# Hybrid SSD / gated-DeltaNet encoder block on one core: SBUF buffers moved to offsets that are multiples of 256 bytes

## What is computed

```python
h = rms_norm(x, g_mix_pre)
proj = h @ w_in                        # 1024 -> 8224 columns: z, xbc, dt, qkv, gate, b, a, m_gate
y_ssm = mamba2_branch(z, xbc, dt, ...)          # causal conv, silu, chunked scan
y_gdn = gdn_branch(qkv, gate, b, a, ...)        # causal conv, silu, l2 norm, chunked delta rule
mixed = sig(mg0) * (y_ssm @ w_br_ssm) + sig(mg1) * (y_gdn @ w_br_gdn)
x = x + rms_norm(mixed @ w_out, g_mix_post)
h = rms_norm(x, g_ffn_pre)
act = gelu(causal_dwconv(h @ w_ffn_gate, conv_ffn_w) + conv_ffn_b)
x = x + rms_norm((act * (h @ w_ffn_up)) @ w_ffn_down, g_ffn_post)
e = sigmoid(x @ w_ple_gate) * (p @ w_ple_proj)
out = x + rms_norm(e, g_ple_post)
```

## Time and profile before

| | |
|---|---|
| median of 3 runs | 2702.46 us (2697.34 to 2707.08) |
| the profiled execution | 2704.22 us, of which the span from first to last instruction 2702.4 us |
| PE busy | 2580.7 us, 95% of the span, 12044 matmuls |
| weight loads (PEld) | 2115.2 us, 78% |
| DVE / ACT / POOL busy | 1468.1 / 531.8 / 1069.9 us |
| DMA | 304.58 MB, 113 GB/s over the span |
| mean granted TensorE clock | 0.98 |

### The profile page before, as it was taken

The page is one execution under the profiler, slowest core; times in us unless marked ns, Lnnn a source line. Parts: engine busy times, 40 slices in busy tenths (PEclk is TensorE's granted clock), DMA queues, the critical chain, the costliest instruction groups (busy, mean ns, idle before and its releaser), DMA issues. The chain is left out here.

```text
span 2702.4 us, 29575 instructions
## 1 busy us (share of the span) xinstructions
PE 2580.7 (95%) x12044; PEld 2115.2 (78%) x12044; DVE 1468.1 (54%) x1172; ACT 531.8 (20%) x550; POOL 1069.9 (40%) x549
## 2 busy tenths in 40 slices
PE   6999999799989999979998799999999999999998
PEld 5888888577778888768876588888888888888776
DVE  4779776234665567731426744444444444444675
ACT  4100101455412323230014200000000000000332
POOL 2334332365435555523365433333333333333353
PEclk8999999899999999999998899999999999999999
DMA  5222222699856575553243211111111111111132
GB/s 200 101 100 87 101 94 78 178 266 289 255 163 204 159 211 163 169 163 133 98 143 101 94 47 47 47 47 47 47 47 47 47 47 49 54 53 62 63 109 101
DMA packets 277598, 304.58 MB, mean 113 GB/s; under 512 B 43837, under 2 KB 241802, under 8 KB 273418
## 3 DMA queue, kind: packets, MB, share of 16 engines
q1 hardware_dynamic: 246778, 249.40, 30.1%
q10 hardware_dynamic: 30736, 54.01, 5.5%
HBM read 216.87 MB, written 86.51 MB: 112 GB/s over the span
## 5 line engine op out<-in xcount | busy, mean ns | idle before, releaser
L440 PE MATMUL ps<-act_hi,w_hi 128*128 128x512 f32 x2288 | 912.9, 399 | 22.6 <-ACT ring_b L920 12.4
L443 PE MATMUL ps<-act_lo,w_hi 128*128 128x512 f32 x2288 | 898.4, 393 | 0.0
L444 PE MATMUL ps<-act_hi,w_lo 128*128 128x512 f32 x2288 | 896.8, 392 | 0.0
L425 POOL TENSOR_SCALAR w_hi<-w_raw 128x1024 fp32r<-128x1024 f32 x219 | 251.7, 1149 | 1429.6 <-PE ps L440 605.4
L427 POOL TENSOR_TENSOR w_lo<-w_raw,w_hi 128x1024 fp32r<-128x1024 f32 x219 | 582.8, 2661 | 18.3
L440 PEld LDWEIGHTS ps<-act_hi,w_hi 128*128 128x128 f32 x2288 | 431.5, 189 | 123.8 <-ACT ring_b L920 15.5
L444 PEld LDWEIGHTS ps<-act_hi,w_lo 128*128 128x128 f32 x2288 | 430.8, 188 | 95.9
L443 PEld LDWEIGHTS ps<-act_lo,w_hi 128*128 128x128 f32 x2288 | 431.6, 189 | 92.6 <-issue 3.4
L2097 DVE TENSOR_TENSOR tile<-ps,tile 128x1024 f32<-128x1024 f32 x112 | 135.7, 1221 | 107.8 <-PE ps L1626 106.5
L2527 DVE SCALAR_TENSOR_TENSOR ring_a<-xin,par,ring_a 128x1024 f32<-128x1024 f32 x108 | 185.1, 1714 | 11.8 <-DVE ring_a L2521 0.3
L1625 PE MATMUL ps<-f_lo,w_hi 128*128 128x512 f32 x480 | 189.1, 394 | 0.0
(11 more groups left out here) (303 smaller groups left out, 2912.6 us busy)
## 6 DMA issues: line engine op xcount, KB each, us to landing
w_raw<-in_w_in_dram SPq DMA_DIRECT2D x34, 1024.0 KB, 5.4
spill<-ring_b ACTq DMA_DIRECT2D x67, 512.0 KB, 2.7
w_raw<-in_w_ffn_gate_dram SPq DMA_DIRECT2D x17, 1024.0 KB, 5.4
w_raw<-in_w_ffn_up_dram SPq DMA_DIRECT2D x17, 1024.0 KB, 5.4
w_raw<-in_w_ffn_down_dram SPq DMA_DIRECT2D x16, 1024.0 KB, 4.9
qkv_a<-spill SPq DMA_DIRECT2D x8, 1536.0 KB, 12.5
dec_a<-cum_rows SPq DMA_DIRECT2D x16, 512.0 KB, 13.9
gdn_in<-hrow SPq DMA_DIRECT2D x8, 1024.0 KB, 11.9
```

Source lines behind the costliest of these rows:

```text
L425: nc.gpsimd.tensor_scalar(hi, raw, 1.0, 0.0, ALU.mult, ALU.add).then_inc(split_done, 1)
L440: first = nc.tensor.matmul(o, wh, mov[0][:, k, c], start=(k == 0), stop=False)
L443: nc.tensor.matmul(o, wh, mov[1][:, k, c], start=False, stop=False)
L444: last = nc.tensor.matmul(o, wl, mov[0][:, k, c], start=False, stop=(k == KD - 1))
```

## The change

Only the order and number of SBUF allocations change; no instruction is added, removed or moved on any engine, apart from the addresses.

1. `w_raw`, `w_hi`, `w_lo` are allocated after the small constants instead of before them; `hv` moves from the head of the mixer's stack to the constants; an unused tensor `fill` of 32 bytes follows.
2. An unused tensor `fill_x` of 224 bytes follows `xin`.
3. `orst` moves from the middle of the chunk loop's buffers to their end.

```diff
@@ -64,14 +64,16 @@
-    w_raw = sb("w_raw", [P, 2, 2048])
-    w_hi = sb("w_hi", [P, 2, 1024], f32r)
-    w_lo = sb("w_lo", [P, 2, 1024], f32r)
     ident = sb("ident", [P, P])
     ones = sb("ones", [P, P])
     eps_t = sb("eps_t", [P, 1])
     par = sb("par", [P, 4, P])
     d_ch = sb("d_ch", [P, KD])
+    hv = sb("hv", [P, 4])
+    fill = sb("fill", [P, 8])
+    w_raw = sb("w_raw", [P, 2, 2048])
+    w_hi = sb("w_hi", [P, 2, 1024], f32r)
+    w_lo = sb("w_lo", [P, 2, 1024], f32r)
@@ -122,7 +124,6 @@
     ph12 = ExitStack()
-    hv = sb("hv", [P, 4], f32, ph12)
     m_incl = sb("m_incl", [P, P], f32, ph12)
@@ -144,6 +145,7 @@
     xin = sb("xin", [P, 2, SEQ + 4], f32, sub)
+    fill_x = sb("fill_x", [P, 56], f32, sub)
     hrow = sb("hrow", [P, 4, SEQ], f32, sub)
@@ -176,12 +178,12 @@
     yssm = sb("yssm", [P, KD, P], f32, ph2)
-    orst = sb("orst", [P, GDN_HEADS], f32, ph2)
     xbc = sb("xbc", [P, XBC_T, P], f32, ph2)
     nt = sb("nt", [P, GDN_HEADS, P], f32, ph2)
     dd = sb("dd", [P, 2 * GDN_HEADS, P], f32, ph2)
     rinv = sb("rinv", [P, GDN_HEADS, P], f32, ph2)
     xinv = sb("xinv", [P, GDN_HEADS, P], f32, ph2)
+    orst = sb("orst", [P, GDN_HEADS], f32, ph2)
```

## The result

The changed kernel takes 2684.34 us (median of 5 runs, 2676.67 to 2688.19) against 2702.70 us of the kernel before in the same session (5 runs, 2697.34 to 2707.08). A later session gave 2679.98 against 2701.77 us.

What follows compares the result with a forecast made beforehand. PE was taken as the bound, busy 2580.7 of 2702.4 us. No instruction is added or moved and every address term was taken as 0, so 2702.5 + 0 = 2702.5 us, range 2692 to 2710.

Steps and rivals of the forecast that it cites:

- PE's reads: Matmul operand reads: new start addresses change nothing, 0 us, with bounds of -176 us and its mirror.
- B: All float32r matmuls: reads run faster at 0 because PE's two reads meet less often, -176 us, 2526; chance 0.03.
- Rival D: Float32r matmuls: slower at 0, with weights and moving operand at one remainder, up to 2879 us; chance 0.02.
- DVE: Convolution taps reading `xin`: offset does nothing, 0 us, all staying at 1283 to 1285 ns.
- ACT and POOL: Operations of these engines: 0 us, lower end -1 us; durations stay with their lines, not with the offset.
- DMA, stores: 512 KB stores out of `ring_b` and `hrow`: 0 us, both landing after 2.6 us whatever the offset.
- DMA, loads: Loads into `xbc`, `gt`, `dec`: taken as 0; a misaligned target costs at most 0.4 of 4.3 us, 9%.
- Rival A: Chunk loop: transfers at remainder 224 pay for it and the change removes that, -9 us, 2693; chance 0.09.
- The seam: Between Z stretch and chunk loop: PE's 7.54 us wait unchanged, 0 us, ends -7.5 and +5.9 us.
- rival C: Seam gets longer: `sub_n` lands 5.9 us later and the clock stays down longer, +9.5 us, 2712; chance 0.06.
- faster: Whole kernel: time measurably below no change, by about 0.3%, 8 us; chance 0.11.

Runs made afterwards that it cites:

- loop_at_0: Kernel before with only the buffers of the epilogue (`ring_a`, `ring_b`, `xin`) and of the chunk loop moved to 0: 2700.46 us, ratio 0.9986.
- the direct comparison above: Changed kernel beside the changed kernel without its 32-byte filler (all buffers at 224), on one chip: 2679.98 against 2687.85 us.

## Why the prediction was wrong, step by step

**The step that failed** is the first term, *PE's reads*: "I take 0: the float32 rows are nearest, being the same engine, the same two reads and the same change of remainder." In its place the runs show 2.22 ns less per float32r matmul, 228.89 to 226.67, set by the difference of the two starts. The nearest rival was B, given 0.03: it had the sign, and a start address as the cause. But its condition, an operand at 0, isn't the one that counts (both at 128 or 224 do as well), its size was off (19 ns per matmul), and that PE's two reads meet, as it said, fits all runs but was not isolated. The row that the prediction named for B showed it: 4148 starts in the 940 us, where "right" was 4108, give or take 3. Three things were wrong in that step.

*The wrong variable.* The step compared remainders (`dd`, `nt` at 0 with `rhs`, `mq` at 224), but each of these pairs has equal remainders, so the difference was 0 in both rows that it compared. They could not show what 64 bytes between the operands cost. Rival D even named the fact ("now at one remainder instead of 64 bytes apart") and gave it the wrong sign. By the runs, in cycles at 2.4 GHz per matmul of 512 columns:

| moving operand minus weights, mod 256 | 0 | 32 | 64 | 96 | 128 | 160 | 192 | 224 |
|---|---|---|---|---|---|---|---|---|
| cycles | 544 | 560 | 549.3 (at times 560) | 560 | 558 or 560, by stretch | 562.3 | 560 | 560 |

So the kernel before was already in the second-best place, and the change brought it to the best.

*The wrong neighbour.* Float32 matmuls are not like float32r ones here. In the trace after, sixteen of either pair still take 1.95 us, and four of 512 columns 1.88, as in the earlier trace rows. One of these rows says more than the prediction took from it: `s_ssm` lay at 224 and `xbc` at 0 and both are at 0 now, so this float32 pair did change its difference, and its time stayed. Other float32 pairs of 512 columns (`hrow`, `ones` and `fa`, `ones`) cover the remaining differences in the traces, 0 to 224 in steps of 32, and take 428.7 to 429.9 ns in the mean at each.

```profile
852.86 1.88 PE L831 MATMUL ps<-s_ssm,xbc 128*128 128x512 f32 x4
...
868.85 1.95 PE L778 MATMUL ps<-rhs,mq 128*128 128x128 f32 x16
...
875.09 1.95 PE L778 MATMUL ps<-dd,nt 128*128 128x128 f32 x16
```

The float32 one spends about 0.43 us on 512 columns, 1.9 times the time of the float32r one, so it takes in its columns at about half the rate.

*A row that was at hand and not read.* The trace of before holds float32r matmuls at both levels of the clock, right behind the seam's wait; start us, us, instruction:

```profile
790.51 0.63 PE L443 MATMUL ps<-act_lo,w_hi 128*128 128x512 f32 x1
790.94 0.63 PE L444 MATMUL ps<-act_hi,w_lo 128*128 128x512 f32 x1
791.37 0.63 PE L440 MATMUL ps<-act_hi,w_hi 128*128 128x512 f32 x1
791.79 0.63 PE L443 MATMUL ps<-act_lo,w_hi 128*128 128x512 f32 x1
792.22 0.63 PE L444 MATMUL ps<-act_hi,w_lo 128*128 128x512 f32 x1
...
792.99 0.39 PE L443 MATMUL ps<-act_lo,w_hi 128*128 128x512 f32 x1
793.22 0.39 PE L444 MATMUL ps<-act_hi,w_lo 128*128 128x512 f32 x1
```

At the lower level, 1.2 GHz (granted clock 0.50 from 790.5 to 792.3 us), four spacings take 792.22 - 790.51 = 1.71 us, 0.427 us each: 512 cycles for 512 columns, nothing on top. At 2.4 GHz it is 549.3 cycles. A clock twice as fast makes the matmul only 1.86 times as fast, so 37 cycles, 15.5 ns, of every matmul were not column work at its rate at the lower level. That is a sign that something other than the array sets the pace, and by it the most that a layout can give is, as an estimate, 9552 * 15.5 ns = 148 us, from a measurement instead of the guessed "half the cost per column". After the change 32 of the 37 cycles are still there. In the kernel with weights at 0 alone, 560 cycles at the upper level, the lower one shows the same 0.427 us (803.91 - 799.64 = 4.27 us for ten):

```profile
799.64 0.63 PE L445 MATMUL ps<-act_lo,w_hi 128*128 128x512 f32 x1
...
803.91 0.63 PE L446 MATMUL ps<-act_hi,w_lo 128*128 128x512 f32 x1
```

In each of the fourteen traces such spacings at the lower level average 425 to 427 ns. So the placement costs only at the upper level. Float32r at the lower level, half as fast, doesn't feel it, nor does float32 at half the speed per column; that the speed of reading is the reason is inferred from these two, not tried by itself.

**DVE: right.** The taps are still at 1283/1285 ns, with `xin` at 0 and 16. **ACT and POOL: right.** The durations stayed with their lines and not with the offset, as the last part of the prediction said: 1057/1061 ns for L2434, now at 0, against 1058/1060 at 224; 1887 ns as `dec_a`'s minimum, 1904 for `s_ssm`, which was 1906 and has moved to 0. The 2% between these two lines belong to the operations.

**DMA, stores: a small effect that the rows were too coarse for.** In the views a store out of `ring_b`, now at 0, lands after 2.6 us, beside 2.6 in the rows of before; over all 67 such stores the median went from 2.7 to 2.6. The time stamps in the traces are finer. Up to 475 us the median is 2.60 us in each of the four profiled executions with `ring_b` at 0, and 2.63 in each of the ten with it at 32, 64, 128, 160, 192 or 224; in the trace of before, the one `hrow` store of the earlier trace rows took 2.59 us, and `ring_b`'s beside it 2.62. So a store takes 0.03 us more wherever it doesn't start at 0, and the prediction's 0 was wrong by that. On the path it is nothing that the runs can tell: `loop_at_0` has the shorter stores, and its ratio is 0.9986 with 1 inside the interval. **DMA, loads: right at this resolution.** `gt` went from 4.3 to 4.1 us, `dec` from 17.3 to 16.9, but `xbc`, which did not move by its remainder, went from 5.9 to 5.3, so changes of this size come without a new remainder.

```profile
spill<-ring_b ACTq DMA_DIRECT2D x67, 512.0 KB, 2.6
...
dec<-cum_rows SPq DMA_DIRECT2D x8, 1024.0 KB, 16.9
...
xbc<-spill SPq DMA_DIRECT2D x8, 768.0 KB, 5.3
```

The Trainium skill, "DMA: Bandwidth & Descriptors", section "How a descriptor splits into AXI transactions", has misaligned descriptors cost extra beats; for `ring_b` that was estimated at 0.1 us. The stores agree in sign, with about a third of the size (2.63 against 2.60 us).

**Rival A** is neither shown nor dead. Its measurable part, the other buffers at 0 alone, gave a ratio of 0.9986 with 1 inside the interval; the direct comparison above leaves 4 to 8 us, about its size, but at a few waits of PE. The loads don't decide it: there `dec` has a median of 16.8 us against 17.1 with all at 224, and `gt` 4.6 against 4.2.

**The seam: right, and rival C didn't come.** The wait went from 7.54 to 8.26 us, within the 2 us that the prediction gave it, where C wanted 13; the clock from 760 to 800 us did fall, from 0.91 to 0.87. `sub_n`'s loads took 7.4 and 7.8 us, not 13.2. PE's waits after:

```profile
PE ps L1130 <- ACT hrow L1192: 12.9, 1, 12.9
...
PE ps L442 <- ACT ring_b L922: 12.6, 4, 8.3
PE ps L442 <- DVE act_lo L1982: 8.5, 5, 3.5
PE ps L886 <- DVE qs L1086: 8.5, 6, 3.1
```

Now the 4 us that the pace should give and the span doesn't have. Some 2 of them never arise. Matched matmul by matmul between the two traces, the 9293 spacings of float32r matmuls without an interruption sum up to 19.1 us less, 2.05 ns each and not 2.22, and the 448 of them in the chunk loop give nothing: in the trace after, the first nine spacings behind an interruption average 229.2 ns (over the 27 runs of at least 24), and 226.7 comes only then. The chunk loop's runs are 3 to 11 spacings long between other work and never get there.

The rest goes in waits and in matmuls at the lower clock. Followed along the order of matmuls, the start of the 2000th is 3.7 us earlier than before and that of the 3200th 6.7, but that of the 3300th only 4.7 and that of the 5200th 2.4; from the 7200th (4.2) on it grows to 16.9, by 9.5 of it in the MLP, which has no waits. Around the seam and in the chunk loop others end last: `ring_b` at the seam, `act_lo` 1.4 us more than the 7.1 before. A faster PE only arrives at them earlier. Likewise the slow layouts lost less than their pace: 9552 * 4.4 ns = 42 us for weights at 0, and the time rose by 32.

**The range and the chances.** Its ends came from rivals A and C, while B, the only term with thousands of instances behind it, was left outside as a whole, because its one price was the 176 us of a guessed bound. A term bounded at 176 us to either side has all values between as well: 5% of that bound, 9 us, is already more than "no change". The range and the chance of "faster" should have contained the small form of B.

## What to carry to other kernels

Let the moving operand and the weights of a float32r matmul start at the same remainder by 256 within their partition (both at 0, 128 or 224 gave 544 cycles, any other difference tried 549 to 562): it costs a few bytes of padding, and in a long unbroken stretch that PE bounds it was worth 1% against the kernel before and 3% against the worst layout. Other shapes and types than float32r with 512 columns weren't tried, float32 apart, where no difference showed. To see whether a matmul stream is held up by anything but its columns, compare its pace at the two levels of the clock in the same trace: a factor of less than two between them (here 1.86) points to such time. And when a row stands in for one that is missing, check that it varies what the change varies, here the difference between two addresses and not the addresses.

## What the hardware showed that was not expected

- The pace of float32r matmuls with 512 columns at 2.4 GHz depends on the difference of two start addresses (544 to 562.3 cycles); at 1.2 GHz it is 512 cycles whatever the layout. Behind an interruption the pace of 544 cycles comes only after some nine matmuls. Float32 ones don't change (1.95 and 1.88 us for the groups shown).
- The Trainium skill, "SBUF — State Buffer", section "Who interferes with whom", calls PE's two reads independent and says that PE waits on no one. For the other engines the runs agree: with DVE busy for 309 of 400 us the pace is that of the stretch where it is busy for 430 of 940. Between the two reads of PE itself they disagree, if those reads are what meets: the difference of their starts is worth 18 cycles of 562.
- At a difference of 64 bytes one layout has two paces, 549.3 and 560 cycles; in the two profiled executions that show both, the pace switched at interruptions of the float32r stream and could switch back (560 from 419 to 485 us, and from 1541 to 2566 us). What decides it is open, as is the origin of the 32 cycles that remain at a difference of 0.
- A 512 KB store from `ring_b` lands after 2.60 us when it starts at 0 and after 2.63 from six other remainders.
